# A decoder step on one core: the background work of a tile laid out over 64 steps, with two steps between producer and consumer

## The reference, cut

```python
def peer_ffn(x, w_q, keys, u_tab, v_tab):
    ...
        q = (xt @ w_q).reshape(PEER_BLOCK, PEER_HEADS, 2, PEER_DK // 2)
        s = jnp.einsum('thcd,hcnd->thcn', q, keys, preferred_element_type=jnp.float32)
        sv, si = lax.top_k(s, PEER_TOPK)
        ...
        top_s, top_p = lax.top_k(cand_s, PEER_TOPK)
        idx = jnp.take_along_axis(cand_i, top_p, axis=-1)
        g = jax.nn.softmax(top_s, axis=-1)
        a = jnp.einsum('td,thkd->thk', xt, u_tab[idx], preferred_element_type=jnp.float32)
        hk = (g * jax.nn.gelu(a, approximate=False)).astype(xt.dtype)
        return jnp.einsum('thk,thkd->td', hk, v_tab[idx])

    for i in range(DEPTH):
        ...
        hp = layer_norm(DN_ALPHA * hp + yp, ln_g[i, 0], ln_b[i, 0])
        hp = layer_norm(DN_ALPHA * hp + peer_ffn(hp, w_peer_q[i], peer_keys[i], peer_u[i], peer_v[i]), ln_g[i, 1], ln_b[i, 1])
        hp = hp + jax.nn.sigmoid(hp @ w_gate) * (p @ w_proj)
```

## Time and profile before

| | |
|---|---|
| three timed executions | 3240.28, 3244.95, 3246.25 us (median 3244.95) |
| profiled execution | 3244.58 us, span 3242.7 us |
| TensorE matmul / weight load busy | 2933.3 us (90%) / 1634.9 us (50%) |
| VectorE busy | 2304.2 us (71%) |
| ScalarE busy | 1271.8 us (39%) |
| GpSimd busy | 1231.2 us (38%) |
| moved by DMA | 1242.82 MB, 383 GB/s over the span |
| mean granted TensorE clock | 0.975 |

### The profile page before, as it was taken

One profiled execution on the slowest core, in us unless ns is written; L12 is line 12 of the kernel. 1 busy time (PEld: TensorE's weight loads), 2 busy tenths in 40 slices (PEclk: granted clock), 3 DMA queues, 4 the chain that ended last, 5 costly groups with the idle time before them and its releaser, 6 DMA issues.

```text
span 3242.7 us, 33343 instructions
## 1 busy us (share of the span) xinstructions
PE 2933.3 (90%) x9278; PEld 1634.9 (50%) x9278; DVE 2304.2 (71%) x5838; ACT 1271.8 (39%) x3559; POOL 1231.2 (38%) x1100
## 2 busy tenths in 40 slices
PE   9998999989877989999898899999899887779998
PEld 7765555545533545555454355555455333334544
DVE  0654677777688788776767777778767888767754
ACT  0143333343334553333433463333334444345642
POOL 0100344444444444343334444334433454444441
PEclk9998999999999999999999999999999999999999
DMA  5514899999999999999899999999999999999996
GB/s 181 208 66 160 332 421 421 421 421 421 421 421 417 399 416 399 421 421 416 366 421 421 421 420 421 421 419 398 421 408 421 406 418 421 421 420 395 421 422 267
DMA packets 179256, 1242.82 MB, mean 383 GB/s; under 512 B 20038, under 2 KB 23366, under 8 KB 32640
## 3 DMA queue, kind: packets, MB, share of 16 engines
q0 software_dynamic: 156896, 1115.93, 83.4%
q1 hardware_dynamic: 22032, 123.73, 9.6%
q10 hardware_dynamic: 144, 1.05, 0.1%
HBM read 1234.16 MB, written 6.50 MB: 383 GB/s over the span
## 4 chain that ended last, share of the span: by engine, by line
PE 43%; DMA 33%; DVE 14%; ACT 4%; issue 2%; DVEq 2%; ACTq 1%; POOL 0%; SPq 0%; POOLq 0%
DMA arena<-in_uv,idx 32%; PE acc L1773 19%; DVE arena L1576 7%; PE bank L1799 6%; PE bank L1808 6%; PE bank L1631 3%; PE bank L1671 2%; PE acc L1782 2%; ACT diag L1164 1%; DVEq L1484 1%; ACT L1142 1%; ACT act_w L1151 1%; DMA arena<-in_uv,small 1%; PE bank L1676 1%; PE bank L1719 1%
## 5 line engine op out<-in xcount | busy, mean ns | idle before, releaser
L1773 PE MATMUL acc<-arena,diag 128*128 128x512 f32 x3864 | 1792.3, 611 | 236.0 <-ACT diag L1164 235.2
L993 POOL DMA_INDIRECT arena<-in_uv,idx x1024 | 1180.2, 1153 | 1646.7 <-PE acc L1773 1311.4
L1576 DVE CUSTOM_DVE_ANT_0 arena<-arena,h 128x1024 f32<-128x1024 f32 x1024 | 1227.6, 1221 | 452.8 <-DMA arena<-in_uv,idx 449.0
L1773 PEld LDWEIGHTS acc<-arena,diag 128*128 128x128 f32 x3864 | 731.2, 195 | 1156.6 <-issue 771.7
L1148 ACT ACTIVATE act_w<-dots 128x2 f32<-128x2 f32 x520 | 105.8, 203 | 1504.0 <-DVE dots L1576 1503.5
L1808 PE MATMUL bank<-hT,panel 128*128 128x264 f32 (+2 forms) x1792 | 405.4, 381 | 10.6 <-ACT hT L1115 6.6
L1808 PEld LDWEIGHTS bank<-hT,panel 128*128 128x128 f32 x1792 | 337.4, 191 | 103.0 <-issue 53.6
L1164 ACT ACTIVATE diag<-cst,act_w 128x128 f32<-128x128 f32 x966 | 336.4, 394 | 52.7 <-PE acc L1773 19.7
L1151 ACT ACTIVATE act_w<-act_w 128x1 f32<-128x1 f32 x1040 | 249.9, 287 | 43.0 <-issue 0.7
L1148 ACT ACT_TABLE_LOAD x127 | 162.9, 1283 | 1.8 <-issue 0.2
L1799 PE MATMUL bank<-panel,qT 128*128 128x256 f32 (+1 forms) x640 | 144.4, 379 | 0.0
(11 more groups left out here) (219 smaller groups left out, 2251.1 us busy)
## 6 DMA issues: line engine op xcount, KB each, us to landing
panel<-in_panels SPq DMA_DIRECT2D x95, 1024.0 KB, 9.1
arena<-in_uv,idx POOLq DMA_INDIRECT x1024, 20.0
arena<-in_cache_k POOLq DMA_DIRECT2D x16, 512.0 KB, 5.7
arena<-in_cache_v POOLq DMA_DIRECT2D x16, 512.0 KB, 5.0
arena<-in_panels SPq DMA_DIRECT2D x6, 1024.0 KB, 7.0
arena<-out_y_s POOLq DMA_DIRECT2D x8, 512.0 KB, 6.4
lng<-in_ln SPq DMA_DIRECT2D x6, 512.0 KB, 12.8
lnb<-in_ln SPq DMA_DIRECT2D x6, 512.0 KB, 16.1
```

The costliest lines, as they stand in the source:

```text
L993: nc.gpsimd.indirect_dma_start(uv[:, slot_of(e), :], None, uv_dram[layer], bass.IndirectOffsetOnAxis(ids[:, r:r + 1], 0)).then_inc(gathere ...
L1576: V.tensor_tensor_reduce(uv[:, slot_of(e), 0:D], uv[:, slot_of(e), 0:D], x_rows, 1.0, 0.0, ALU.mult, ALU.add, dots[:, G % 2, r:r + 1]).the ...
L1773: m = mm(acc[:, half * 512:(half + 1) * 512], diag[:, r % DIAGS, :], uv[:, slot_of(e), D + half * 512:D + (half + 1) * 512], start=False, ...
```

## The change

The lots are made for 64 steps at once, and `window_pairs` no longer cuts a coarse lot by its number of pieces. Where a piece has `fence`, or where the first `turn` of a row comes, the list goes on two steps of the 64 after the piece before it (before: one coarse step, that is two of the 64, and two coarse steps behind a `norm_b`; and a coarse lot was cut into halves afterwards, so that the distance could come out as one step). The gap behind `stage` is gone. Behind each gap the rest of the list is spread anew over what is left of the lane (before, all went by one line over the whole lane, and what the gap had pushed back caught up at once). Four lanes get other ends, and the norms of tiles 0 and 1 at the end of layer 1 move from coarse steps 30 to 32 of window 1 and 2 to 6 of window 2 to 24 to 28 of window 2.

```diff
-            lots = [[] for _ in range(4 * HEADS if b < TB else 2)]
+            lots = [[] for _ in range(8 * HEADS if b < TB else 4)]
             for first, last, pieces in lanes:
-                total, so_far = sum(COST[x.kind] for x in pieces), 0
-                at, before = first, None
+                rest, so_far = sum(COST[x.kind] for x in pieces), 0
+                at, base, before = 2 * first, 2 * first, None
                 for x in pieces:
-                    if before and (x.fence or x.kind == "turn" and before != "turn" or before == "stage"):
-                        at = min(at + (2 if before == "norm_b" else 1), last - 1)
-                    at = max(at, first + int(so_far * (last - first) / total))
+                    if before and (x.fence or x.kind == "turn" and before != "turn"):
+                        at = min(at + 2, 2 * last - 1)
+                        base, rest, so_far = at, rest - so_far, 0
+                    at = max(at, base + int(so_far * (2 * last - base) / rest))
                     lots[at].append(x)
                     so_far += COST[x.kind]
                     before = x.kind
...
-        window(0, 2, (3, 22, r3), (22, 32, rs[:13]), (0, 32, early))
+        window(0, 2, (2, 22, r3), (22, 32, rs[:13]), (0, 32, early))
...
-        tile0, tile1 = self.norm(3, (0,), True), self.norm(3, (1,), True)
-        window(1, 1, (0, 11, r1[17:]), (19, 32, r2[:25]), (0, 30, late), (30, 32, tile0))
+        norms = self.norm(3, (0,), True) + self.norm(3, (1,), True)
+        window(1, 1, (0, 11, r1[17:]), (19, 32, r2[:25]), (0, 30, late))
         side, spread = self.sample_rows(1)
-        window(1, 2, (0, 4, r2[25:]), (4, 24, rs), (24, 25, side), (26, 27, spread), (25, 32, r3[:9]), (2, 6, tile1))
+        window(1, 2, (0, 4, r2[25:]), (4, 23, rs), (23, 24, side), (25, 26, spread), (27, 32, r3[:9]), (24, 28, norms))
...
 def window_pairs(layer, b, lots):
 
     first = first_group(layer, b)
-    out = []
-    for t, lot in enumerate(lots):
-        cut = (len(lot) + 1) // 2
-        for half, part in enumerate((lot[:cut], lot[cut:])):
-            out.append((2 * t + half, first + t // 2, 2 * (t % 2) + half, t // 4, part))
-    return out
+    return [(t, first + t // 4, t % 4, t // 8, lot) for t, lot in enumerate(lots)]
```

## The result

The changed kernel takes 3250.4 us (median of 8 runs, 3248.2 to 3252.4), the kernel before 3242.7 (8 runs, 3238.4 to 3246.25): a ratio of 1.0024 with a 95% interval of 1.0015 to 1.0033. It is 0.24% slower, clear of the interval. I had said 3229, 16 us faster, in a range of 3219 to 3249. The profiled execution has a span of 3247.7 us.

The account below looks back on a forecast made before the run. The prediction took DMA at its 421 GB/s ceiling as the bound, shortened only where engines run dry: 21.6 us won, 3.5 and 2 given back, net 16, so 3244.95 - 16 = 3229 us, range 3219 to 3249.

Parts of the forecast that it names:

- The bursts and what makes them: Five DMA dips (1210 to 2951 us) follow back-to-back TensorE products made by the old layout; they hold 20.4 us.
- The rival that the bursts are not the cause of the dips: Panel loads or the ring's state make the dips, so they stay: 3245 us, chance 0.08.
- Nothing in the change alters a byte, so this part can only be shortened where the DMA engines run dry: From the sixth slice on, DMA at 421 GB/s is a ceiling; dips between 380 and 3190 us hold 23.6 us.
- Won: 20.4 + 1.2: Gain of 21.6 us: 20.4 from the dips of five bursts, 1.2 from the dip at 2560 us.
- The 9.6 us at 1585: Layer 0, tile 3: loss of 7.2 + 2.4 us after a 5.4 us wait and 48 products, to be won back.
- Given back: doubles 3.5 us, keys and short waits 2: Costs set against the gain: five doubles at 0.7 us each, 2 us for earlier keys and new short waits.
- The keys' wait: Before layer 1's first key scores, one step earlier: TensorE stands about 5 us (4 to 10); cost 0, bound 3.
- The doubles: Five places where a joined step and its follower still put 32 matmuls back to back: 0.7 us each, 3.5 us.
- In the first window the order is nearly the old: 0.: Layer 0, tile 0: the new lane ends and route order there cost nothing, 0 us.
- Norms moved: 0 to 1.2 us of gain: Layer 1, norms of tiles 0 and 1 leave the routes near 2560 us: cost 0, gain 0 to 1.2 us.
- The slower rival: Six turns two steps behind a `norm_b` make TensorE wait, then start products late: 3259 to 3270 us, chance 0.12.
- The tail: End of the kernel: the 55 us behind the last gather, the last tile's own chain, stay the same.

Follow-up runs that it names:

- e6: Kernel before with the new layout only in layer 0's tile 3, keys' load in step 34: 3242.7 us (0.9999).
- e10: Kernel before, its 80 panel loads behind 380 us without the last quarter of every row, 21 MB less: 3194.9 us (0.9845).
- e2: Changed kernel with the old coarse layout in the first window (layer 0, tile 0) alone: 3242.7 us (0.9997).
- e5: e2 with the `stage` piece, which issues the load of layer 1's keys, in step 34 instead of 40: 3243.9 us (1.0000).
- e1: Changed kernel with the gap behind `stage` given back, first key scores in step 42 and not 41: 3251.2 us (1.0026).
- e7: Kernel before with the new layout in the first window (layer 0, tile 0) only: 3249.8 us (1.0026).
- e3: Changed kernel with only `root` of the first window moved back from lot 1 to lot 0: 3245.5 us (1.0006).
- e8: e2 with the norms of layer 1's tiles 0 and 1 in their old places: 3242.5 us (1.0000).
- e13: Kernel before, its 80 panel loads behind 380 us without partitions 0 to 31, 21 MB less: 3358.1 us (1.0358).

## Why the prediction was wrong

*The bursts and what makes them.* Right for the most part. No row of 32 or 48 products stands behind the turns of layer 0's tile 3, four rows of 32 are left elsewhere, 32 adds are joined (128 matmuls of L1778), and four of the five dips went with their bursts, as e6 shows for one window alone. The last window's dip at 2920 stayed without its burst. The rival that the bursts are not the cause of the dips is wrong, though its 3245 us is, by luck, about what a kernel without the first window's fault takes. TensorE was not the limit: e10 shows that DMA was. The Trainium skill, "Trainium Kernel Development and Optimization", section Performance Expectations, says that matmul busy time is a bad metric of how close a kernel is to its roofline and weight-load busy a good one. The runs agree in that TensorE had room: e10 has the same TensorE instructions in 48.2 us less.

*"Nothing in the change alters a byte, so this part can only be shortened where the DMA engines run dry", and "Won: 20.4 + 1.2".* The step that failed. The share is a mean over 16 engines. One landing record of the 16 lags by up to 15 us, and VectorE waits for it. In a dip that record catches up with the rest. The 9.6 us at 1585 were such a dip (spread 11.7 to 3.7 us), and the other eight are smaller, each less than the lag at its place. The whole term measures 0: e2 has the new layout behind the first window, and takes 3242.7 us for 3243.25. Added up over all stretches from 480 to 3160 us, the dips are 24.8 us in before, 18.8 in e2 and 14.8 in e5, and these three take the same time.

*Given back: doubles 3.5 us, keys and short waits 2.* The keys' wait was mis-sized, 12.15 us for about 5, and its dip with 8.4 us is larger than the bound of 3. It cost nothing all the same, by e1 and e5, for the same reason: in e2 the spread falls there from 15.3 to 2.2 us. The doubles were not priced alone; e2 as a whole is even, so they cost nothing that can be seen.

*"In the first window the order is nearly the old: 0."* The second step that failed, and the one that decides the sign. The order of the pieces was nearly the old, but not their steps. `root` stood one lot before `factors`, which needs it, and the new lots put both into one; both turns were put to four products of the same lot. I had listed the places of gates, queries or turns in five windows, and in this one none. It measures 7.2 us (e7), 4.9 of it through `root` (e3). Which of the turns, the shared lot of the norm or the earlier queries makes the rest, no run separates. The dip itself is (0.92 - 0.83) x 40 + (1.01 - 0.97) x 40 = 5.2 us, and here it counts in full, since the spread is 1 to 3 us; the 2 us above it are not explained.

*Norms moved: 0 to 1.2 us of gain.* 0 (e8). The dip at 2560 went and gave nothing, and by e8 it went for another reason than the norms.

*The slower rival.* I had put the loss at a short distance behind `norm_b`, at six places. It was elsewhere and by another mechanism: two pieces on different engines that need each other, in one lot.

*The tail.* As predicted, about 55 us behind the last gather.

So 16 us of gain were 0, and a cost of 0 was 7.2; 3242.7 (the eight runs' median of before) + 7.2 is 3249.9, measured 3250.4.

## To carry to other kernels

Before a dip in a mean DMA share is counted as time to be won, look at when the last of the transfer's landing records comes, and whether that one moves; in this kernel a dip no larger than the lag of the last record was worth nothing, and what lay beyond it counted. Where no such lag had built up, as near the start, a dip of 5 us cost 7. When a schedule is spread over a finer grid, check each pair of pieces that hand over between engines (here `root` and `factors`), above all in the window where no stock is in hand yet, rather than the kinds of piece whose costs were the reason for the change.

## What the runs showed of the hardware that was not expected

- One of the sixteen landing records of a gather falls behind the rest while DMA is full. In before its median lag behind the fifteenth is 0.1 us at 380, 3.4 at 620, about 6 at 860 and 9.2 at 1060; after the dip at 1585 it is 1.8, and then it grows again to 6.8 at 2180. Why is open. One engine may also carry instruction loads: queue 8 (kind "instruction") has 74 packets of 16 KB, 15 of them between 380 and 1060 us. In the trace they take 1.07 us each, 16 us in all, where the lag grew by 9.1. That they make the lag is not shown.
- A load of 96 partitions costs more than one of 128: 80 of them made the kernel 118 us slower (e13), with DMA's share at 1.01 and 360 to 416 GB/s in most slices. Rows shortened by a quarter instead (e10) gave 48 us back. Packets take longer while such a load and a gather overlap (485 ns for 312), and why is open.
- A share of 1.01 alone is thus no sign of full rate: the GB/s beside it have to be read too.
- The load of the keys, 1 MB, took 1669.3 - 1658.7 = 10.6 us from issue to use while gathers filled the engines, and TensorE stood all that time.
